# DMA crossbar transposes in place of TensorE transposes for 24 token tiles of a hybrid decoder trunk

## The reference

```
def layer_norm(x, g, b):
    mu = mean(x); var = mean((x - mu)^2)
    return ((x - mu) * rsqrt(var + 1e-5)) * g + b
def swiglu(x, w_gate, w_up, w_down):            # D_FF = 2816
    return (silu(x @ w_gate) * (x @ w_up)) @ w_down

x = layer_norm(ALPHA * x + 0.5 * swiglu(x, f1_wg, f1_wu, f1_wd), ln_f1_g, ln_f1_b)
z = x @ w_in + b_in                             # 1024 -> 2560 columns
a_val, a_gate, g_b, g_c, b_val = split(z)       # 512 each
u  = a_val * sigmoid(a_gate)                    # group A
ua = silu(layer_norm(causal_conv31(u) + b_dw_a, ln_conv_g, ln_conv_b))
ub = g_b * causal_conv3(g_c * b_val)            # group B
x = layer_norm(ALPHA * x + concat(ua, ub) @ w_o + b_o, ln_mix_g, ln_mix_b)
x = layer_norm(ALPHA * x + 0.5 * swiglu(x, f2_wg, f2_wu, f2_wd), ln_f2_g, ln_f2_b)
```

## Time and profile before

| | |
|---|---|
| median of 3 runs | 1214.66 us (1214.13 to 1214.91) |
| the profiled execution: its own time, first to last instruction of the slowest core | 1213.0 us (cores 1209.9 to 1213.0) |
| PE busy | 1190.2 us, 98% |
| DVE busy | 540.5 us, 45% |
| ACT busy | 241.5 us, 20% |
| POOL busy | 197.2 us, 16% |
| DMA, share of the 16 engines by the weight loads' queue / by SP's queue | 42.8% / 18.7% |

### The profile page before, as it was taken

How to read it: one execution, slowest core, us unless ns; L and a number is a source line. 1 busy time by engine, 2 the same in 40 slices (tenths; PEclk the granted TensorE clock), 3 DMA queues, 4 the chain that set the end, 5 groups by cost and what they waited for, 6 DMA issues and landing times.

```text
span 1213.0 us, 19792 instructions; the slowest of 8 cores (1209.9 to 1213.0 us)
## 1 busy us (share of the span) xinstructions
PE 1190.2 (98%) x7131; PEld 632.4 (52%) x7230; DVE 540.5 (45%) x895; ACT 241.5 (20%) x429; POOL 197.2 (16%) x308
## 2 busy tenths in 40 slices
PE   7999999999999999999999999999999999999997
PEld 3544444455555566555444444445444466666444
DVE  1223216663433455727854434455736532222356
ACT  1111110121122245321021121235330011111000
POOL 1111112310101012322210100113412110000111
PEclk8999999999999999999999999999999999999999
DMA  9797877776655538995346656438994244543032
GB/s 193 113 189 125 140 145 151 149 155 119 113 106 103 126 62 174 198 214 151 105 111 108 119 99 128 99 85 170 196 185 152 99 104 76 85 71 88 21 109 104
DMA packets 64368, 152.80 MB, mean 126 GB/s; under 512 B 7760, under 2 KB 24464, under 8 KB 64000
## 3 DMA queue, kind: packets, MB, share of 16 engines
q0 software_dynamic: 34592, 79.21, 42.8%
q1 hardware_dynamic: 29680, 72.32, 18.7%
HBM read 202.79 MB, written 28.70 MB: 191 GB/s over the span
## 4 chain that ended last, share of the span: by engine, by line
PE 96%; DMA 2%; issue 1%; DVE 0%; POOL 0%; ACT 0%; DVEq 0%; ACTq 0%; POOLq 0%
PE ps L538 50%; PE ps L602 24%; PE ps L690 12%; PE ps L942 5%; PE ps L794 2%; DMA sb_xT<-xta 2%; PE ps L413 1%; PE ps L620 1%; PE ps L911 1%; PE ps L880 1%; PE ps L608 0%; DVEq L166 0%; ACT sb_mv L498 0%; POOL sb_xT L1096 0%; PE ps L934 0%
## 5 line engine op out<-in xcount | busy, mean ns | idle before, releaser
L538 PE MATMUL ps<-sb_xT,sb_ring 128*128 128x352 bf16 (+3 forms) x3544 | 630.9, 336 | 8.9 <-DVE sb_dummy L341 3.3
L538 PEld LDWEIGHTS ps<-sb_xT,sb_ring 128*128 128x128 bf16 x3584 | 349.0, 98 | 272.5 <-issue 13.4
L545 DVE TENSOR_TENSOR sb_hT<-sb_sg,ps 128x352 bf16<-128x352 f32 (+3 forms) x224 | 128.8, 576 | 407.8 <-PE ps L538 389.7
L602 PE MATMUL ps<-sb_RW,sb_hT 128*128 128x512 bf16 x1335 | 293.4, 379 | 1.8 <-issue 0.5
L602 PEld LDWEIGHTS ps<-sb_RW,sb_hT 128*128 128x128 bf16 x1364 | 132.8, 98 | 158.1 <-issue 0.2
L543 ACT ACTIVATE sb_sg<-ps 128x352 f32<-128x352 f32 (+3 forms) x224 | 113.6, 507 | 486.2 <-PE ps L538 437.3
L690 PE MATMUL ps<-sb_xT,sb_wring 128*128 128x512 bf16 (+1 forms) x780 | 145.2, 336 | 1.2 <-issue 0.2
L351 POOL DMA_DIRECT2D sb_ring<-wgu x87 | 48.0, 552 | 471.3 <-PE ps L538 412.6
L690 PEld LDWEIGHTS ps<-sb_xT,sb_wring 128*128 128x128 bf16 x800 | 67.8, 97 | 74.7 <-issue 0.8
L443 POOL TENSOR_SCALAR sb_mv<-sb_mv 128x1 f32<-128x1 f32 (+1 forms) x50 | 44.5, 891 | 351.1 <-DVE sb_mv L441 351.1
L435 DVE SCALAR_TENSOR_TENSOR sb_xr<-sb_xr,ps 128x1024 f32<-128x1024 f32 x47 | 57.3, 1219 | 97.8 <-PE ps L602 77.5
(11 more groups left out here) (93 smaller groups left out, 486.1 us busy)
## 6 DMA issues: line engine op xcount, KB each, us to landing
sb_ring<-wgu POOLq DMA_DIRECT2D x87, 512.0 KB, 7.2
sb_RW<-wd POOLq DMA_DIRECT2D x33, 512.0 KB, 13.4
sb_wring<-win POOLq DMA_DIRECT2D x40, 256.0 KB, 5.9
sb_RW<-uscr SPq DMA_DIRECT2D x64, 135.0 KB, 6.1
sb_xr<-xp SPq DMA_DIRECT2D x16, 512.0 KB, 9.1
x1s<-sb_xr SPq DMA_DIRECT2D x16, 512.0 KB, 4.0
sb_xr<-x1s SPq DMA_DIRECT2D x16, 512.0 KB, 10.3
x2s<-sb_xr SPq DMA_DIRECT2D x16, 512.0 KB, 8.9
```

Source lines behind the costliest of these rows:

```text
L538: ins = e.matmul(bank(bk, n), lhsT=ring[:, s, c:c + 128], rhs=xT[:, k, tok0:tok0 + n], start=(k == 0), stop=(k == KC - 1))
L545: P.op("dve", lambda e: e.tensor_tensor(out=hT[:, f, l0:l0 + n], in0=sg[:, q, :n], in1=bank(bu, n), op=ALU.mult), reads=[("sg", q)] + pst( ...
L602: ins = e.matmul(ps[:n, (yb + h) * 512:(yb + h + 1) * 512], lhsT=hT[:, f, l0:l0 + n], rhs=wd[:, f, h * 512:(h + 1) * 512], start=(f == 0), ...
```

## The change

Two sorts of tiles are no longer transposed by `xpose`: the 8 prompt tiles of block 1's first down phase, and the 16 prompt tiles of the two mixers. For them SP issues a DMA with `transpose=True` from `xb` straight into `xT`, one for each tile. In the down phase it is issued when `xb` is made (ahead of the tile's store), in the mixers right after the cast, one step earlier than the transpose stood. Tile 16 and block 0's first down phase keep `xpose`. The `while` loop in `down` now leaves nothing in `pend` for block 1.

```
+        def xpose_dma(t, c):
+            (tok0, n) = tok(t)
+            P.op("sp", lambda e: e.dma_start(out=xT[:, :, tok0:tok0 + n], in_=xb[:n, c, :], transpose=True),
+                 reads=[("xb", c)], writes=[("xT", t)], dma="xd%d" % c)
...
-                while len(pend) > (1 if late is None else 0) and not final:
+                pend[:] = [p for p in pend if p is not None]
+                while len(pend) > (0 if b == 1 else 1 if late is None else 0) and not final:
                     xpose(*pend.pop(0), tb())
...
                     if not final:
                         c = ln_tail2(ctx)
+                        if b == 1 and t < 16:
+                            xpose_dma(t, c)
                         store_xr(t, slots[i], spill(0, t), [("x1", t)])
-                        return (t, c)
+                        return None if b == 1 and t < 16 else (t, c)
...
-                for k in at(i, 5, True):
-                    xpose(tl[k], xbs[k], mb())
                 for k in at(i, 4, True):
                     xbs[k] = cast_xb(tl[k], xslot[k])
+                    xpose_dma(tl[k], xbs[k])
...
-            side.append((lambda: [xpose(*p, cb5()) for p in pend], 1.0))
+            side.append((lambda: [xpose(*p, cb5()) for p in pend if p is not None], 1.0))
```

## The result

The changed kernel takes 1275.89 us (median of 4 runs, 1265.91 to 1288.77) against 1214.79 for the kernel before on the same chip (4 runs, 1214.13 to 1215.59). The ratio is 1.0475 (95% interval 1.0443 to 1.0506): some 58 us slower, where 3.5 us faster was predicted. The kernel before varies by under 2 us from run to run, the changed one by over 20, and so do its cores: in the profiled execution they end between 1241.7 and 1287.2 us. That execution is the longest of the four, the cores of one die ran slower in it than those of the other, and the ratio leaves it out (the medians alone differ by 61 us); so it is read on core 0, of the die that was not disturbed (1249.9 us, clock 0.980), against core 0 of before (1213.0 us, clock 0.995). What is said of "the mean core" is the mean over the eight.

A forecast was written before the change was run, and what follows sets the result against it. PE, busy for 98% of the span, was taken to bound the kernel. The terms gave 1213.0 - 11.3 + 5.1 + 1.7 + 1.0 = 1209.5 us, and the median's 1.66 us above the profiled execution made 1211.2 us; range 1206 to 1232.

The forecast's parts named there:

- The transposes that go: Down phase and mixers: 24 tiles' transposes leave PE at 0.45 us each, plus 0.5 us for ACT's copy: -11.3 us.
- Tile 16's wait: Block 1's down phase: PE asks for tile 16 one down tile earlier and waits for DVE: +5.1 us.
- The clock behind it: After PE's wait before tile 16: PE runs at half clock for a time, as at start-up: +1.7 us (lower bound 0).
- The gather of tile 16: Down phase: tile 16's four small DMAs come later behind tile 10's transfer on SP's queue: +1.0 us (0 to 8).
- Tile 15 at the mixer's start: Start of the mixer: tile 15's transfer, taken as 5 us, fits 6.2 us of room: 0 (0 to 3.4, with clock 5.1).
- The `xb` buffers in the mixers: Mixers: a cast waits for an earlier tile's transfer, which has 10 us and just fits: 0 (0 to 12 each place).
- SP gains 24 issues: SP's queue: added issues and waits for ACT's casts cost nothing while a transfer is issued at once.
- The casts hold ACT: Rival, mixers of units 1 and 3: slow transfers hold casts and Silus; 1229.7 us, past 1240 at 23 us; chance 0.28.
- Late at the mixer's start: Rival: tile 15's transfer takes 9.6 us, PE waits 3.4 us and the clock takes 1.7: 1216.3 us; chance 0.13.
- The rules on the crossbar's speed: Crossbar transfers: one rule gives 1309 ns a block, sum near 1217; another, as fast as ordinary transfers, sum unchanged.

The follow-up runs named there:

- e8: Kernel before, with only tiles 8 to 14 of block 1's down phase by crossbar transfers, tile 16's transposes at their old place: 1213.68 us, ratio 0.9974.
- e9: Kernel before, with tiles 0 to 6 and 8 to 14 of both down phases by crossbar transfers, tile 16 at its old place: 1211.4 us, ratio 0.9946.
- e1_down: Changed kernel with the mixers' 16 tiles back on TensorE, the down phase's 8 tiles still by crossbar transfers: 1246.02 us, ratio 1.0254.
- e5: Changed kernel with each of the 24 transfers a plain copy in 256-byte pieces, without transposing: ratio 1.0234.
- e6: Changed kernel with each of the 24 transfers a plain store to HBM in 128 rows of 2 KB: 1230.8 us, ratio 1.0112.
- e7_small_after: Changed kernel with the SwiGLU weight loads cut into smaller packets: 1249.53 us, ratio 1.0265; its control, the kernel before with the same packets: 1224.1 us, ratio 1.0051.
- e_actq: Changed kernel with ACT, not SP, issuing the crossbar transfers on a queue of its own: 1319.49 us, ratio 1.0819.
- e3: Kernel before, with the 8 tiles of block 1's down phase by crossbar transfers, mixers on TensorE, tile 16's transposes at their old place: ratio 1.0003.
- e2_mixers: Changed kernel with the down phase put back as before, only the mixers' 16 tiles by crossbar transfers: 1271.68 us, ratio 1.0455.

## Why the prediction was wrong, step by step

- **The transposes that go, -11.3 us.** Right where it was tested, in the down phases: e8 and e9 gained 3.2 us for 7 tiles and 6.6 us for 14 tiles, 0.46 and 0.47 us a tile, where the earlier trace rows gave 0.45. No run shows the gain of the mixers' 16 tiles, or the 0.5 us for ACT's copy, by itself.
- **Tile 16's wait, +5.1 us.** Right in place and size: 5.0 us in e1_down on each of the eight cores, and on core 0 of e5, e6 and e7_small_after (4.9 in e_actq). In the changed kernel it is 9.2 on core 0: DVE began the phase late, its first tile at 562.32 after 20.9 us of waiting for xp, and worked tile after tile without a break, so tile 16 came later still.
- **The clock behind it, +1.7 us.** In part. Six cores of e1_down end where the terms put them (on core 0 the clock is 0.65 from 586 to 592 us, just behind the wait: 6 x 0.35 = 2.1 us); the others lose 30 us to the granted clock of 0.81. The one dip of the start-up was no bound for what a wait can do to the clock, and the range given for this term (0 to 1.7) had no upper end worth the name.
- **The gather of tile 16, +1.0 us.** Not seen: with 5.0 us, e1_down leaves nothing for it.
- **Tile 15 at the mixer's start, 0 (0 to 3.4).** In the range: 0 to 1.8 us in e1_down, 2.1 on core 0 of the changed kernel, up to 2.8 in e3. The slowest of the down phase's transfers lands in 7.0 to 8.4 us, against 6.2 of room.
- **The `xb` buffers in the mixers, "By the stores ... it just fits: 0".** This step failed. The transfer was sized by its 256 KB against the store's 512 KB; at the end of unit 1 the four land in 12.7 to 28.1 us (median 17.7), against 10 of room, and ACT's casts wait 8.8 us for transfers on core 0, 17.1 by the mean core. "The 24 transfers move 6 MB, little beside the 152.8 MB" measured them in bytes, where e5 to e7 show that the crossbar and the size of the packets on both queues weigh more. The row that it should have been nearest to was the 23.0 us of queued loads, which stood in the range.
- **"SP gains 24 issues ... cost nothing while a transfer is issued at once".** This failed more dearly, for this is the way by which the loss came. The text named what stands behind the transfers (stores and loads) and then priced only ACT's casts. On core 0 PE waited 3.1 us for ACT in the mixers (8.0 by the mean core). DVE waited 40.7 us for x1s (at the products that write the token of `gate`) and 20.9 for xp behind the transfers, and PE 26.1 for DVE (28.6 by the mean core). The condition "issued at once" didn't hold either: issues held SP for up to 16.07 us, and the hold of 15.66 us stands in the chain in front of xp.
- **The rivals.** "The casts hold ACT" (0.28, 1229.7 us, past 1240 at 23 us) had the long transfer and its place right, and a part of the way by which it reached PE (8.0 us by the mean core), but missed the larger part, over the loads and DVE, and so came to 15 us over the kernel before (25 at its worst) where 58 were measured. "Late at the mixer's start" is real but small. The range ended at 1232, and the measured 1275.9 is far outside: its upper end was built from one wait in each of two places, with nothing for a queue whose delays add up.
- **The rules on the crossbar's speed.** Eight blocks land in 3.0 to 3.1 us when the engines are quiet, 0.39 us a block, so the 1309 ns a block of the Trainium skill ("VectorE: DVE Perf Modes", "The three transpose paths") is not what a tile costs eightfold here. Its other rule ("Advanced Engine Details and Errata", "X-Bar Transpose (TRN2)": as fast as ordinary DMAs) agrees with the quiet stretches, 3.0 us against 2.9 for the plain copy in 256-byte pieces. Beside the weight loads it doesn't hold: e5's plain copies make the kernel 0.0241 x 1214.8 = 29 us faster than the crossbar's.

## What to carry to other kernels

Size an added DMA by its packets, and by the packets that it meets there on other queues, not by its bytes: 1056 packets of 256 bytes were 3 us in a quiet stretch and 18 to 22 us beside weight loads. Then go through everything that stands behind it on its queue, loads above all, and price each as late by that much, at whatever waits for it, tokens that carry no data included; an engine that issues a DMA can itself be held. A move off a full engine pays only where the transfer has slack on both sides: 7 of the change's 24 tiles had it, and with 7 more of the other down phase they gave 6.6 us, while its 16 in the mixers cost 55 us by themselves (e2_mixers, 0.0455 x 1214.8).

## What the hardware showed that was not expected

- Issuing a crossbar transfer takes 1.25 us of SP's queue (the plain copy of the same pieces 0.6, the 2 KB rows 0.32), and up to 16 us while the one before is still under way: the hold of 473.64 us ends at 489.71, and the transfer before it (466.86, 23.5 us to landing) lands at 490.4. On ACT's queue it is up to 13.1 us, in which ACT does nothing else. A plain copy in nearly as many pieces was held for 3.1 us at most on any core.
- Cutting the packets of *another* queue to a quarter halves the transfer's time (22.1 to 11.3 us) though that queue keeps the engines busier over the run, and costs 6 us by itself in a kernel without such transfers (1.0051).
- After one wait of 5.0 us, some cores of e1_down were granted a clock of 0.81 for some 150 us with PE busy, which costs 30 us, and others none; a wait of the same length in three other kernels (e5 to e7) had no such effect. The cause is open.
